# Summing equal weight tiles on VectorE ahead of one narrow product, in the mLSTM stage of a hybrid decoder

## What is computed

```python
w_intra = jnp.einsum('bhtd,bhsd->bhts', q, k) * jnp.exp(logD - m_t[..., None])
num = jnp.einsum('bhts,bhsv->bhtv', w_intra, v) + ...        # the numerator
den = jnp.sum(w_intra, axis=-1) + ...                         # the sum of the same weights
h = num / jnp.maximum(jnp.abs(den), jnp.exp(-m_t))[..., None]
```

## Time and profile before

| | |
|---|---|
| time, median of three runs | 1765.58 us |
| lowest and highest of them | 1760.44 and 1770.26 us |
| the profiled execution: its time, its span | 1764.44 us, 1762.9 us |
| mean granted TensorE clock over the span | 0.95 |
| TensorE, VectorE, ScalarE, GpSimd busy | 93%, 47%, 27%, 17% |
| TensorE instructions | 12277 |
| VectorE instructions | 1497 |
| the edited stage, by the timeline | about 249 to 309 us of the span |

### The profile page before, as it was taken

How to read it: one execution, slowest core, us unless ns; L and a number is a source line. 1 busy time by engine, 2 the same in 40 slices (tenths; PEclk the granted TensorE clock), 3 DMA queues, 4 the chain that set the end, 5 groups by cost and what they waited for, 6 DMA issues and landing times. The chain is left out here.

```text
span 1762.9 us, 30817 instructions
## 1 busy us (share of the span) xinstructions
PE 1636.8 (93%) x12277; PEld 1515.7 (86%) x12277; DVE 820.8 (47%) x1497; ACT 483.5 (27%) x747; POOL 292.8 (17%) x370
## 2 busy tenths in 40 slices
PE   6999989888989999999999899997599999999996
PEld 5999965666668999999999799973498999999996
DVE  4332453644546634444222867327657443443225
ACT  3111321444434322222111422135234222222121
POOL 1411000400000334343000200001302333332000
PEclk8999988888999999999999999988599999999998
DMA  4232150677351132333322132211220323233311
GB/s 136 76 97 65 43 149 1 204 222 238 101 177 49 49 95 76 90 91 94 99 70 89 48 116 73 84 48 54 74 72 25 95 71 95 74 101 99 89 43 51
DMA packets 225261, 159.76 MB, mean 91 GB/s; under 512 B 17882, under 2 KB 206022, under 8 KB 225177
## 3 DMA queue, kind: packets, MB, share of 16 engines
q1 hardware_dynamic: 221896, 156.78, 30.6%
q0 software_dynamic: 3280, 1.85, 0.5%
HBM read 148.98 MB, written 9.88 MB: 90 GB/s over the span
## 5 line engine op out<-in xcount | busy, mean ns | idle before, releaser
L2176 ACT CAST w_high<-ring 128x1024 fp32r<-128x1024 f32 (+1 forms) x148 | 165.5, 1118 | 740.1 <-PE psum L1977 716.0
L1977 PE MATMUL psum<-mixed_high,w_high 128*128 128x280 f32 x1472 | 310.3, 292 | 15.0 <-DVE mixed_low L2373 13.0
L1977 PE MATMUL psum<-mixed_high,w_low 128*128 128x280 f32 x1472 | 312.1, 293 | 0.0
L1977 PE MATMUL psum<-mixed_low,w_high 128*128 128x280 f32 x1472 | 309.5, 292 | 0.0
L2365 DVE TENSOR_TENSOR w_low<-ring,w_high 128x1024 fp32r<-128x1024 f32 (+1 forms) x148 | 237.1, 1602 | 136.1 <-ACT w_high L2176 136.1
L1977 PEld LDWEIGHTS psum<-mixed_high,w_high 128*128 128x128 f32 x1472 | 235.6, 189 | 16.0 <-DVE w_low L2365 13.7
L1977 PEld LDWEIGHTS psum<-mixed_high,w_low 128*128 128x128 f32 x1472 | 236.2, 190 | 0.0
L1977 PEld LDWEIGHTS psum<-mixed_low,w_high 128*128 128x128 f32 x1472 | 233.8, 189 | 0.0
L2581 POOL TENSOR_TENSOR silu<-silu,rstd 128x560 f32<-128x560 f32 x44 | 61.3, 1393 | 606.3 <-DVE silu L2445 606.3
L2445 DVE TENSOR_TENSOR silu<-silu,psum 128x280 f32<-128x280 f32 x88 | 35.3, 443 | 156.2 <-PE psum L1977 154.6
L343 PE MATMUL psum<-normed_high,w_high 128*128 128x280 f32 x448 | 94.3, 292 | 0.8 <-PEq L530 0.8
(11 more groups left out here) (491 smaller groups left out, 3201.7 us busy)
## 6 DMA issues: line engine op xcount, KB each, us to landing
ring<-in_ffn_wd SPq DMA_DIRECT2D x16, 1408.0 KB, 7.0
ring<-in_ffn_wg SPq DMA_DIRECT2D x40, 512.0 KB, 4.0
ring<-in_ffn_wu SPq DMA_DIRECT2D x40, 512.0 KB, 5.2
ring<-in_w_in_even SPq DMA_DIRECT2D x14, 1024.0 KB, 5.4
ring<-in_w_in_odd SPq DMA_DIRECT2D x12, 1024.0 KB, 5.3
ring<-in_cache_fox_k SPq DMA_DIRECT2D x44, 256.0 KB, 4.4
projected<-in_cache_fox_v SPq DMA_DIRECT2D x28, 256.0 KB, 2.9
projected<-in_cache_fox_k SPq DMA_DIRECT2D x20, 256.0 KB, 3.9
```

Source lines behind the costliest of these rows:

```text
L1977: done = mm(banks[2 * tl + a][:, 0:HALF], w, m[a], start=first and s == 0, stop=last and s == 2)
L2176: nc.scalar.copy(dst, src).then_inc(w_hi[p], 1)
```

## The change

In range 1, the narrow products of blocks 0 to 3 go. VectorE adds their weight tiles to a buffer `wsum` of 272 columns, in a part of the weight ring that is not in use in this stage: at b = 1 the tiles of b = 0 and 1 are added, at b = 2 and b = 3 the tile of that block is added to the sum, in its own columns (`at` is 0 or, for b = 3, 128). Each addition follows a drain. The addition for b = 3 increments a new semaphore, `d_ws`. TensorE waits for it at b = 3, behind the wait for that tile's weights, and then does one narrow product of 272 columns with the sum. Range 0, blocks 4 and 5 of range 1, and the retention layer stay as they are.

```diff
-    d_s, d_w, d_wu, d_numc = (sem(x) for x in ("scores", "weights", "weights_used", "num_copied"))
+    d_s, d_w, d_wu, d_numc, d_ws = (sem(x) for x in ("scores", "weights", "weights_used", "num_copied", "weights_summed"))
+    wsum = ring[:, 1, 1280 + 2 * T:1280 + 2 * T + 272]
...
                     stop = final and b != SB
-                    if mlstm:
+                    if mlstm and r and b == 3:
+                        pe.wait_ge(d_ws, hd + 1)
+                        nc.tensor.matmul(banks[7][0:4, 0:272], onecol[:, hd, :], wsum, start=(hd == 0), stop=False,
+                                         skip_group_check=True)
+                    if mlstm and (not r or b >= 4):
                         nc.tensor.matmul(banks[6 + r][0:4, c0:c0 + w], onecol[0:n, hd, :], wbuf[i % 4][0:n, 0:w],
                                          start=(first and hd == 0), stop=(stop and hd == MH - 1), skip_group_check=True)
...
                     v.tensor_tensor(wbuf[i % 4][0:n, 0:w], banks[2 + i % 2][0:n, 0:w], dec, ALU.mult).then_inc(d_w, 1)
+                    if mlstm and r and 1 <= b <= 3:
+                        at = t0 - 256
+                        v.drain()
+                        last = v.tensor_tensor(wsum[:, at:at + w], wbuf[(i - 1) % 4][:, 0:w] if b == 1 else wsum[:, at:at + w],
+                                               wbuf[i % 4][:, 0:w], ALU.add)
+                        if b == 3:
+                            last.then_inc(d_ws, 1)
                     if between is not None and i % 2:
                         between(dve, i // 2)
```

## The result

The changed kernel took 1780.04 us (median of 5 runs, 1772.29 to 1781.99) where the kernel before took 1763.33 on the same chip: a ratio of 1.0081, interval 1.006 to 1.0102. Timed once more in ten runs it took 1773.63 us against 1764.05, ratio 1.005, interval 1.0033 to 1.0066. It is slower, by 10 to 17 us; the forecast was 0.7 us faster, and both medians lie above the range.

What follows compares the result with a forecast made beforehand. TensorE is busy 93% of the span, but VectorE's order was taken to pace the edited stretch. Heads 0 to 2 gain 0, head 3 0.69: 0.7 us less, 1763.7 from the profiled execution, stated as 1764.9; range 1759.0 to 1771.5.

Steps and rivals of the forecast that it cites:

- The order on VectorE: Edited stage, per head: additions of 0.44, 0.44 and 0.31 us behind drains; each full-width one holds the order 0.53 us more.
- w(3) to num(5): Tile 3's weight multiplication to tile 5's third product, each head: about 4.6 us in heads 0 to 2, 3.9 in head 3.
- The gain of 0.69 us in head 3: Last head, with no exponents for a next head: tile 5's third product starts 0.69 us earlier; heads 0 to 2 gain 0.
- The new waits: TensorE waits for the sum behind tile 6's score; later products, ScalarE's copies and tile 7's weights queue behind, no DMA moves.
- rival (1): Edited stage: TensorE's pauses make the clock fall before the state products; 6.1 us slower, 1771.7; chance 0.14, including 0.02 for 1776.5.
- the clock term of the forecast: Edited stage: the 0.7 us forecast includes no cost from an earlier clock fall; this forecast case has chance 0.76.
- the point that the prediction set for this rival: Deciding sign in the edited stage: granted clock below 1.00 ahead of a head's state products.
- the row that spoke against the rival: Retention layer, same loop without narrow products: clock stays 1.00 in the matching stretch of 2.33 us, though TensorE doesn't pause there.
- The price, 6.1 us: Clock falling earlier: 3.41 us more at half clock per head costs 1.7, 6.8 in four heads; less 0.7, 6.1 slower.
- Rival (2): Edited stage: TensorE sets the pace because additions cost VectorE's order less; up to 6.1 us faster, 1759.5; chance 0.10.
- The range: Whole kernel: 1759.0 to 1771.5 us, the runs' spread of some 5 us either way, a little further up for the clock.

Runs made afterwards that it cites:

- f1: The changed kernel with two unread products filling only TensorE's longer pause, ahead of the sum's product; 1769.96 us, ratio 1.0033 to the kernel before.
- g4: The kernel before, all narrow products kept, plus VectorE additions each done three times, their sum unread; 1783.72 us in four runs, ratio 1.0115.
- e1: The changed kernel without additions, drains and the wait for the sum; its one narrow product reads a tile's weight buffer; 1760.81 us, ratio 0.9982 to the kernel before.
- e3: The changed kernel with unread products issued into both TensorE pauses, one in the first and two in the second; 1766.81 us, ratio 1.0004 to the kernel before.
- e0: The changed kernel unaltered, run again for a second trace; 1773.63 us, ratio 1.005 to the kernel before; its profiled execution took 1781.75 us.

## Why the prediction was wrong

**The order on VectorE: right.** The additions took 0.44 and 0.31 us; three narrow products less and one of 272 columns are 24 instructions less (12277 to 12253 on the page). Head 1's timeline in after, against the earlier trace rows:

```profile
274.67 0.44 DVE L1198 TENSOR_TENSOR projected<-psum,projected 128x272 f32<-128x272 f32 x1 [0.48 <-PE psum L1089]
275.20 0.44 DVE L1202 TENSOR_TENSOR ring<-projected 128x272 f32<-128x272 f32 x1
275.56 0.50 DVE L1172 TENSOR_SCALAR projected<-psum,gate_columns 128x272 f32<-128x272 f32 x1
...
276.39 0.44 DVE L1198 TENSOR_TENSOR projected<-psum,projected 128x272 f32<-128x272 f32 x1
276.89 0.72 PE L1116 MATMUL psum<-projected,token_major 128*128 128x272 f32 x2 [0.64 <-DVE projected L1198]
276.92 0.44 DVE L1202 TENSOR_TENSOR ring<-ring,projected 128x272 f32<-128x272 f32 x1
...
277.99 0.31 DVE L1198 TENSOR_TENSOR projected<-psum,projected 128x144 f32<-128x144 f32 x1
278.39 0.31 DVE L1202 TENSOR_TENSOR ring<-ring,projected 128x144 f32<-128x144 f32 x1
278.84 0.62 PE L1111 MATMUL psum<-ring,small 128*4 128x272 f32 x2 [1.08 <-DVE ring L1202]
279.39 0.39 PE L1116 MATMUL psum<-projected,token_major 128*128 128x144 f32 x1
```

w(4) and w(5) no longer wait for their scores. The first two additions start 0.53 us after their w, worked out as 0.52, and the exponents 0.36 later, as worked out. From w(3) to num(5) it is 4.72 us, forecast 4.61; in head 3 4.05, forecast 3.93. What TensorE saves it spends waiting, as the prediction said. The gain of 0.69 us in head 3 came to 0.57.

**The new waits: half right.** The wait for the sum, 1.08 us, was in the prediction with what is queued behind it. Its size stood only in rival (1), which put TensorE's pauses at over a third of the stretch; measured are 0.64 + 1.08 of 4.72 us. The 0.64 us for w(4) was not named as a pause of TensorE; f1 shows that it counts.

**The failed step: the clock term of the forecast, put at nothing, and with it rival (1), its chance and its price.** The forecast let TensorE wait at no cost beyond the stretch itself. But the clock fell ahead of every head's state products, which is the point that the prediction set for this rival, and it had only 0.14. It rested on retention's 1.00 with no narrow products while TensorE there doesn't pause, as the prediction itself noted; the row that spoke against the rival couldn't bear on it. The edited stage runs at half clock in three places before the change already (two of them in the earlier trace rows): a stretch that lies that near to a fall was the reason to ask what pauses of 0.64 and 1.08 us in 4.7 would do, and the prediction gave the case in which they do nothing 0.76. g4, with pauses and no work taken out, shows that pauses bring the clock down; e1, with the work taken out and no pauses, shows no fall ahead of the state products; e3, with the pauses filled, takes the loss back.

The price, 6.1 us, was too small, and for a reason that can be named. It let 3.41 us more run at half in each head, 13.6 us in all. Measured are 46.5 - 24.1 = 22.4 us more in the profiled execution (by a clock column rounded to 0.01). By the line, 22.4 / 2 us of lost clock over a span of 1771 are 0.0063 of clock, times 1350 us gives an estimate of 8.5 of the 9.3 us. The stretch that the prediction took as the measure was the shortest; what was added is 6.8 us behind each of heads 0 and 1, 3.4 behind head 2, and 5.0 within the stage around and behind head 3's state products.

**The size of a loss of clock.** The table's line says 1.35 us for each 0.001 of mean clock, for the kernel before; the runs of the other kernels, taken together, have nearly the same slope (1.37). The change in its ten runs lies 0.006 under the kernel before, 8.1 us, and 1.6 us off the line: together about the 9.6 us measured. In the first five it lies 0.009 under it, 12.2 us and 1.9 off the line, 14 of the 16.7 us; the clock is given to 0.001. This is the clock of the whole span, so it holds the later stages too, which the second trace (e0) shows to differ as well. Those 1.6 to 1.9 us at an equal clock the prediction had as 0.7 us of gain. Of the difference the stretch w(3) to num(5) makes 0.8 (18.59 - 18.47 = 0.1 more, forecast 0.69 less); what makes the other part stays open.

**Rival (2)** was right for the worth of the products, 6.0 us in e1 at an equal clock, and wrong for the change: that TensorE's pace sets the end needs weights that come in time. **The range** took in the clock only up to 1771.5, just under that rival's own 1771.7.

The Trainium skill, TensorE: Matmul & The Clock Gate, the section on psum-queue depth-cycling, told of short idle times between groups of products that send the clock back and forth at a cost. The runs agree: 0.64 and 1.08 us of idle time, clock 0.83 to 0.71 in the stage. The prediction cited it and gave it too little weight beside a row that couldn't test it. The Trainium skill, VectorE: DVE Perf Modes, section Terms, has the next operation wait for an empty pipe; the trace of after speaks against it as that of before did, since the exponents at 275.56 start 0.08 us before the addition at 275.20 has ended (275.64).

**Open:** the share of each pause, for f1's runs lie in two groups; the share of the work taken out beside that of the pauses (e1's clock); why the same kernel's executions differ in clock by up to 0.012 (the kernel before ran between 0.940 and 0.952), in e0's trace mostly behind the edited stage; and whether the change with its pauses closed by useful wide products would keep e1's 6 us, which wasn't tried.

## What to carry to other kernels

Taking work off an engine that is busy all the time pays only if what feeds it is in time; cut the stretch out and follow the feeder's order before counting the saving. Where TensorE's clock falls somewhere in the stage already, a new pause of a microsecond in a dense stretch may cost time even if it holds up no later work, as it did here: look at what runs next, above all thin products, and price it at half clock. One trace shows one execution: before its stage clock is read, see where its time lies among the runs. When two versions are compared, set their times against their mean granted clocks: the distance from the common line is the change itself, the place along it is the clock.

## What the runs showed of the hardware

- Over 87 executions of one kernel, time follows the mean granted clock with a scatter of 1.2 us: 1.35 us per 0.001.
- Sixteen instructions of state products of four columns take 1.95 us at a clock of 1.00 and 3.58 at 0.50.
- TensorE kept at work by products that nobody reads made the changed kernel faster: 1766.81 against 1773.63 us.
- With all products kept, pauses of up to 1.07 us lowered the median granted clock from 0.949 to 0.942 (g4, four runs).
- A VectorE multiplication with both operands in SBUF took 0.81 and 0.88 us instead of 0.28 while GpSimd added 272 columns (0.76 us).
- Twelve additions of 0.31 to 0.44 us on VectorE cost nothing measurable where TensorE didn't wait for them (ratio 0.9988).
